# The conditioning products of an eight-head hybrid decoder step, moved from split and plain fp32 on the whole array to plain fp32 on four column strips

## The reference, cut to what matters

```python
def adaln(c, w_ada, b_ada):
    m = jnp.einsum('nd,de->ne', jax.nn.silu(c), w_ada) + b_ada
    return tuple(jnp.split(m[:, None, :], 6, axis=-1))
```

## Time and profile before

| | us |
|---|---|
| median of 3 runs | 1800.78 (1799.39 to 1802.48) |
| the profiled execution, its own time | 1803.02 |
| its span in the trace | 1801.2 |
| PE busy in the span | 1689.8 (94%) |
| DVE, ACT, POOL busy | 1010.5, 739.8, 479.3 |
| stage 1, from the span's start | 0 to 71.8 |
| stage 2 | 71.8 to 294.4 |

### The profile page before, as it was taken

How to read it: one execution, slowest core, us unless ns; L and a number is a source line. 1 busy time by engine, 2 the same in 40 slices (tenths; PEclk the granted TensorE clock), 3 DMA queues, 4 the chain that set the end, 5 groups by cost and what they waited for, 6 DMA issues and landing times. The chain is left out here.

```text
span 1801.2 us, 27774 instructions
## 1 busy us (share of the span) xinstructions
PE 1689.8 (94%) x11308; PEld 1565.1 (87%) x11308; DVE 1010.5 (56%) x1730; ACT 739.8 (41%) x1365; POOL 479.3 (27%) x304
## 2 busy tenths in 40 slices
PE   5799997889999999998999998999999999999997
PEld 2699995788877887876998988999999999999896
DVE  2411113735567877774436464222789778888535
ACT  3311222334555655652324354210474456436511
POOL 0454442100000000000125472221333443434621
PEclk9899997789999999999899999999999999999998
DMA  9254433512111001012562032112020202020422
GB/s 303 66 132 110 106 98 108 152 32 58 38 48 40 29 28 39 29 36 90 171 192 71 36 107 71 36 48 94 12 94 25 71 25 71 25 71 15 139 71 60
DMA packets 174668, 137.16 MB, mean 76 GB/s; under 512 B 44245, under 2 KB 160129, under 8 KB 174505
## 3 DMA queue, kind: packets, MB, share of 16 engines
q1 hardware_dynamic: 166827, 125.16, 23.5%
q10 hardware_dynamic: 7718, 10.29, 1.7%
HBM read 115.82 MB, written 21.92 MB: 76 GB/s over the span
## 5 line engine op out<-in xcount | busy, mean ns | idle before, releaser
L2653 PE MATMUL ff_acc<-x_ring,w_ring 128*128 128x258 f32 x3360 | 407.8, 284 | 3.2 <-DVE x_ring L2954 3.2
L2653 PEld LDWEIGHTS ff_acc<-x_ring,w_ring 128*128 128x128 f32 x3360 | 407.4, 191 | 3.7 <-POOL w_ring L2470 3.0
L2470 POOL TENSOR_TENSOR w_ring<-w_quads,w_ring 128x512 fp32r<-128x512 f32 x90 | 162.5, 1807 | 275.7 <-ACT w_ring L2235 275.6
L1257 PE MATMUL gate_ps<-h_hi,gate_w_cut 128*128 128x344 f32 x768 | 228.5, 346 | 7.4 <-ACT gate_sum L1380 5.1
L2235 ACT ACTIVATE w_ring<-w_quads 128x512 fp32r<-128x512 f32 x140 | 88.1, 629 | 177.1 <-PE ff_acc L2653 86.0
L1257 PEld LDWEIGHTS gate_ps<-h_hi,gate_w_cut 128*128 128x128 f32 x768 | 142.5, 194 | 14.5 <-ACT gate_sum L1380 7.7
L1353 ACT ACTIVATE prob<-scores,bias 128x640 f32<-128x640 f32 (+7 forms) x192 | 106.0, 558 | 99.3 <-DVE bias L1421 50.2
L1448 DVE TENSOR_TENSOR p_lo<-pT,p_hi 128x512 fp32r<-128x512 f32 (+1 forms) x148 | 101.4, 686 | 69.6 <-ACT p_hi L1364 69.1
L1364 ACT ACTIVATE p_hi<-pT 128x512 fp32r<-128x512 f32 (+1 forms) x148 | 88.1, 595 | 99.5 <-PE pT L1307 98.6
L1257 PE MATMUL gate_ps<-h_lo,gate_w_cut 128*128 128x344 f32 x384 | 125.0, 325 | 0.0
L1559 POOL MEMSET qz<- 128x576 f32 x1 | 0.6, 582 | 467.3 <-POOLq L130 467.3
(11 more groups left out here) (424 smaller groups left out, 3922.4 us busy)
## 6 DMA issues: line engine op xcount, KB each, us to landing
w_quads<-in_w_ff_dram SPq DMA_DIRECT2D x20, 1024.0 KB, 5.3
wa_rest<-in_w_ada_dram SPq DMA_DIRECT2D x16, 1024.0 KB, 5.3
gate_spill<-gate_sum SPq DMA_DIRECT2D x48, 172.0 KB, 1.9
gates<-gate_spill SPq DMA_DIRECT2D x16, 516.0 KB, 4.9
wa<-in_w_ada_dram SPq DMA_DIRECT2D x8, 1024.0 KB, 9.8
gate_w_raw<-in_w_in_dram SPq DMA_DIRECT2D x16, 512.0 KB, 4.1
ff_raw<-in_w_ff_dram SPq DMA_DIRECT2D x16, 512.0 KB, 4.1
w_raw<-in_w_in_dram SPq DMA_DIRECT2D x30, 256.0 KB, 6.3
```

What stands on the lines that cost most here:

```text
L1257: last = pe.matmul(gps[:, 0:CH], gw_cut[:, 1 - u % 2, a, k], h[:, k, c * CH:(c + 1) * CH], start=(k == 0 and n == 0), stop=(k == KD - 1 an ...
L2470: pool.tensor_tensor(wr[:, n % HK, 1], quad_piece(ph, W_PART[name], p), wr[:, n % HK, 0].bitcast(F32), ALU.subtract).then_inc(wrest_pool, 1)
L2653: last = pe.matmul(banks[:, 2 * p + c, 0:HC], wr[:, n % HK, a, k], xr[:, jj % 2, b, k, c * HC:(c + 1) * HC], start=(fresh and k == 0 and m ...
```

## The change

Both stages multiply `w_ada` in the same way now, in `strip_products`: plain fp32, with the stationary block padded with zeros from 9 to 32 columns (`c_pad`), and the 8 inner blocks spread over four strips of 32 array columns, two blocks to a strip. Strip s holds the sum of blocks 2s and 2s + 1 in PSUM rows 32s to 32s + 31. The order is: the first block of strips 0, 1, 2, 3, then the second block of strips 0, 1, 2, 3. What the rows' turning multiplies with is a new `fold`, 128 x 9, with a one wherever the row's number modulo 32 is the column's, so that the turning product adds the four strips. Stage 1 turns with this product instead of a transpose. In stage 2 the cuts of `w_ada` on ACT and POOL are gone, and the products wait for the chunk's landing itself.

```diff
+        c_pad = buf.at("c_padded", [P, KD, STRIP], F32, buf.tail + 2 * AC * 4)[0]
+        fold = buf.const("fold", [P, 1 + NS])
+        def strip_products(pe, acc, w_chunk):
+            per = KD // NSTRIP
+            for half in range(per):
+                for strip in range(NSTRIP):
+                    k, row = strip * per + half, strip * STRIP
+                    last = pe.matmul(acc[row:row + STRIP], c_pad[:, k], w_chunk[:, k], start=(half == 0), stop=(half == per - 1),
+                                     skip_group_check=True, tile_position=(0, row))
+            return last
...
-                        for k in range(KD):
-                            last = pe.matmul(adaP[c % 2][:], cT[:, k], wa[:, c % NR, k], start=(k == 0), stop=(k == KD - 1))
+                        last = strip_products(pe, adaP[c % 2], wa[:, c % NR])
...
-                        last = pe.transpose(tp[0][:, n * 16:n * 16 + 1 + NS], arow[:, n * P:(n + 1) * P], ident[0:1 + NS, 0:1 + NS])
+                        last = pe.matmul(tp[0][:, n * 16:n * 16 + 1 + NS], arow[:, n * P:(n + 1) * P], fold[:], start=True, stop=True,
+                                         skip_group_check=True)
...
-                    dve.tensor_copy(cT[:], tp[0][:, 0:KD * 16].rearrange("p (k n) -> p k n", k=KD)[:, :, 0:1 + NS]).then_inc(cT_ready, 1)
+                    dve.memset(c_pad[:, :, 1 + NS:STRIP], 0.0)
+                    dve.tensor_copy(c_pad[:, :, 0:1 + NS], tp[0][:, 0:KD * 16].rearrange("p (k n) -> p k n", k=KD)[:, :, 0:1 + NS]).then_inc(cT_ready, 1)
                     dve.wait_ge(consts_ready, 1)
+                    dve.tensor_reduce(fold[:], ident[:].rearrange("p (s c) -> p c s", s=NSTRIP)[:, 0:1 + NS], AX.X, ALU.add)
...
-                pe.wait_ge(walo_ready, c + 1)
+                pe.wait_ge(wa_loaded[c % 2], 16 * (c // 2 + 1))
                 if c:
                     pe.wait_ge(arow_ready, c)
-                else:
-                    pe.wait_ge(cst_ready, 1)
-                for k in range(KD):
-                    pe.matmul(adaP[:], c_st[:, k], wa_hi[:, k], start=(k == 0), stop=False, skip_group_check=True)
-                    last = pe.matmul(adaP[0:1 + NS], c_st[:, k, 0:1 + NS], wa_lo[:, c % 2, k], start=False, stop=(k == KD - 1),
-                                     skip_group_check=True)
+                last = strip_products(pe, adaP, wa[:, c % 2])
...
-            def cut_ada_hi(act, c):
-                act.wait_ge(wa_loaded[c % 2], 16 * (c // 2 + 1))
...
-            def cut_ada_lo(pool, c):
-                pool.wait_ge(wahi_ready, c + 1)
...
-                    dve.wait_ge(chi_ready, 1)
-                    dve.tensor_tensor(c_st[:, :, 1 + NS:NC2], cT[:], c_st[:, :, 0:1 + NS].bitcast(F32), ALU.subtract)
-                    dve.tensor_tensor(fold[:], ident[0:NC2, 0:1 + NS], ident[0:NC2, 1 + NS:NC2], ALU.add).then_inc(cst_ready, 1)
```

More of the change, by code:

```diff
@@ L282, in hybrid_step @@
         AC = 256
-        cT = buf.const("cT", [P, KD, 1 + NS])
+        STRIP = 32
+        NSTRIP = P // STRIP
+        c_pad = buf.at("c_padded", [P, KD, STRIP], F32, buf.tail + 2 * AC * 4)[0]
[8 more added lines that the diff above has]
+            return last
         with ExitStack() as st:
@@ L290, in hybrid_step @@
             htmp = at("htmp", [P, 4, 512])
-            arow = at("arow", [1 + NS, 2 * D])
+            arow = at("arow", [P, 2 * D])
             sq = at("sq", [P, D])
@@ L298, in hybrid_step @@
             tp = [psum(st, f"tp{i}", [P, 512]) for i in range(3)]
-            adaP = [psum(st, f"adaP{i}", [1 + NS, AC]) for i in range(2)]
+            adaP = [psum(st, f"adaP{i}", [P, AC]) for i in range(2)]
             vec_loaded, c_loaded, xs_loaded = sem("vec_loaded"), sem("c_loaded"), sem("xs_loaded")
@@ L525, in hybrid_step @@
             NA = 4 * D // AC
-            wa_at = at.at[0] - buf.CONSTS - 2 * buf.SLAB
             wa = at("wa_rest", [P, 2, KD, AC])
-            NC2 = 2 * (1 + NS)
-            c_st = at("c_st", [P, KD, NC2], F32R)
-            fold = at("fold", [NC2, 1 + NS])
             assert at.at[0] <= buf.CONSTS + 5 * buf.SLAB
-            wa_lo = buf.slabs(2, wa_at)("wa_rest_lo", [P, 2, KD, AC], F32R)
-            wa_hi = buf.slabs(5, 3 * 8192)("wa_rest_hi", [P, KD, AC], F32R)
             behind_arow = buf.tail
-            arow = buf.small("arow_rest", [NC2, 2, AC])
+            arow = buf.small("arow_rest", [P, 2, AC])
             buf.tail = behind_arow
-            adaP = psum(st, "ada_rest", [NC2, AC])
+            adaP = psum(st, "ada_rest", [P, AC])
             adaT = psum(st, "ada_turned", [P, AC // P, 1 + NS])
@@ L540, in hybrid_step @@
             ada_done, arow_ready, adaT_done, ada_taken = (sem(n) for n in ("ada_rest_done", "arow_rest_ready", "ada_rest_turned", "ada_rest_taken"))
-            wahi_ready, walo_ready, chi_ready, cst_ready = (sem(n) for n in ("wa_rest_hi_ready", "wa_rest_lo_ready", "c_hi_ready", "c_st_ready"))
             def condition(pe, c):
-                pe.wait_ge(walo_ready, c + 1)
+                pe.wait_ge(wa_loaded[c % 2], 16 * (c // 2 + 1))
                 if c:
                     pe.wait_ge(arow_ready, c)
-                else:
-                    pe.wait_ge(cst_ready, 1)
-                for k in range(KD):
-                    pe.matmul(adaP[:], c_st[:, k], wa_hi[:, k], start=(k == 0), stop=False, skip_group_check=True)
-                    last = pe.matmul(adaP[0:1 + NS], c_st[:, k, 0:1 + NS], wa_lo[:, c % 2, k], start=False, stop=(k == KD - 1),
-                                     skip_group_check=True)
+                last = strip_products(pe, adaP, wa[:, c % 2])
                 last.then_inc(ada_done, 1)
@@ L563, in turn_ada @@
                 last.then_inc(adaT_done, 1)
-            def cut_ada_hi(act, c):
-                act.wait_ge(wa_loaded[c % 2], 16 * (c // 2 + 1))
-                if c:
-                    act.wait_ge(ada_done, c)
-                act.activation(wa_hi[:], wa[:, c % 2], ACT.Copy).then_inc(wahi_ready, 1)
-            def cut_ada_lo(pool, c):
-                pool.wait_ge(wahi_ready, c + 1)
-                pool.tensor_tensor(wa_lo[:, c % 2], wa[:, c % 2], wa_hi[:].bitcast(F32), ALU.subtract).then_inc(walo_ready, 1)
             with nc.Block() as block:
@@ L605, in _ @@
                 def _(act):
-                    act.activation(c_st[:, :, 0:1 + NS], cT[:], ACT.Copy).then_inc(chi_ready, 1)
-                    cut_ada_hi(act, 0)
                     for u in range(NU):
@@ L610, in _ @@
                             g.cut_hi(act, u // 2 + 1, u % 2)
-                        cut_ada_hi(act, u + 1)
                 @block.gpsimd
                 def _(pool):
-                    cut_ada_lo(pool, 0)
                     for u in range(NU):
@@ L618, in _ @@
                             g.cut_lo(pool, u // 2 + 1, u % 2)
-                        cut_ada_lo(pool, u + 1)
                 @block.tensor
```

## The result

The changed kernel takes **1778.52 us** (median, 1776.71 to 1780.35) against 1800.88 beside it (1799.39 to 1802.48): ratio 0.9876, 95% interval 0.9861 to 0.989, so 22.4 us less. The profiled execution's span went from 1801.2 to 1778.5.

A forecast was written before the change was run, and what follows sets the result against it. PE was taken to bound stage 2 and the stretch of stage 1 from 29.03 to 49.91 us. Stage 1 -3.2, loop +6.9 and tail -6.7 gave -3.0 us: 1797.8 against the median 1800.78, range 1780 to 1815.

The forecast's parts named there:

- u: Stages 1 and 2: cost of one chunk's products in strips including switching, put at 2.32 us, ends 1.94 and 2.51.
- the loop, 15 units, strips: Stage 2, chunks 0 to 14: products rise from 1.86 to 2.32 us each, 15 x 0.46 = +6.9 us on PE's path.
- the loop, turning over 128 rows: Stage 2: row-turning product keeps its instructions, two products, four passes, 0.52 us, only with 128 rows instead of 18.
- stage 1: Before stage 2: last chunk ends 6.3 us earlier, turning takes 3.1 longer, sum -3.2 us; -5.3 if the clock stays up.
- tail: End of stage 2: PE no longer waits for POOL, but SP is late next; 12.08 - 5.36 = -6.7 us.
- What strips make of it: Strip products: matmuls start in program order, so a chunk takes nine steps of 0.216, 1.94 us, before switching.
- the two bounds, 1.18 and 3.45: A chunk's 16 passes in strips: 1.18 us if all four strips run at once, 3.45 if nothing runs side by side.
- The switch: Stage 2, between whole array and strips: drains and a short exposed load, 0.38 us a chunk, from nothing to 0.57.
- all at once: Rival, chance 0.27: each strip queues its own passes, a chunk costs 1.46 us; -19.0 us, 1781.8.
- loads exposed: Rival, chance 0.13: a strip's second load waits for its first pass, a chunk costs 3.18 us; +13.7 us, 1814.5.
- nothing side by side: Rival, chance 0.15: fp32 passes hold the whole array, a chunk costs 3.83 us; +27.3 us, 1828.1.
- The forecast's own case: Stage 1 with chunk 2 at the lower clock: eighth load released at 35.0, last chunk ends at 43.6; case chance 0.45.

## Why the prediction was wrong

The forecast was -3.0 us; measured -22.4. By its own steps:

| step | forecast | measured | from |
|---|---|---|---|
| u, a chunk's products | 1.86 to 2.32 | 1.86 to 1.00, and 0.10 behind it | timeline after |
| the loop, 15 units, strips | +6.9 | -10.2 | 15 x (13.59 - 12.91) |
| the loop, turning over 128 rows | 0 | -3.9 | 14 x (13.87 - 13.59) |
| stage 1 | -3.2 | -0.1 (to -2.6 in other profiles) | start of stage 2: 71.87, 71.79, 69.29 |
| tail | -6.7 | -6.73 | copy 14 to next stage: 12.33, 5.60 |

In the two profiles: the next stage starts 21.35 us earlier (294.41 to 273.06), of which 14.62 stood by the copy of chunk 14 and 6.73 came behind it; the rest of the span, 1506.8 and 1505.4, is 1.4 shorter. That makes the 22.7 between the spans. The table's rows make 20.9 of the 21.35; the other 0.4 lies in the first unit, which has no turning behind it and leaves the lower level a little sooner after than before.

**The step that failed** is "What strips make of it": PE's matmuls were taken to start in program order across strips, because every row before shows it, and every row before used the array as one. From the two bounds, 1.18 and 3.45, the step went to 1.94 by that order. The runs show that the strips keep only their own order: four rounds of 0.216, 0.86 us without the ends. The lower bound itself was 0.32 too high, since it took the spacing of issue, 0.064 a pair, from the transposes; four passes start within 0.04 us here.

**The switch** was set at 0.38 a chunk. It is 0.14, with 0.10 in the unit behind it, and nearly the same stands where nine columns take the place of strips. Had u been right but for this term, the time would have been 15 x 0.14 = 2.1 us off. (By the forecast's own terms u = 1.94 gives a sum of -8.7, not one below it.)

**The rival "all at once"** had the mechanism, strips that queue their own passes, and 1781.8: 3.3 us above the result. That it came so near in time is luck: its loop, -6.0 against some -14.5, lacked the turning's 3.9 and the smaller u, and its stage 1, -6.3, was too good by 6.2. The rivals "loads exposed" and "nothing side by side" fall with u: the loads lie under the passes though all strips use all rows. Two rules of the Trainium skill (TensorE: Matmul & The Clock Gate, "Part 3: Packing small matmuls — row/col tiling"), strict order of start and overlapping loads only where row groups differ, don't hold here: passes of later strips start ahead of earlier strips' second ones, and 16 loads of 0.11 cost nothing within 1.00.

**The turning** was costed at nothing ("keeps its instructions"). The row for the other price stood among those read, the 0.21 of "issue" before the 18-row load; it was not asked why it was there, nor whether 128 rows would keep it.

**Stage 1.** The eighth load went out at 32.6, as the prediction had it for a clock that stays up, but its chunk began 9.0 us later instead of 6.7 (7.4 to 8.1 in six other profiles with four strips in stage 1 and its turning at the end). The forecast's own case had the load out at 35.0 and landed at 41.7; that the chunk began at 41.62 is luck, two errors that cancel. The forecast saw that PE would wait for it and not what the wait does: the clock at 0.50 through the turning, 6.99 us instead of 4.2. It took 3.1 of added turning where 5.8 came. The start of stage 2 varies by 2.5 us between profiles with this stage 1, with the landing of the last chunk and with the level at which its products run.

**The tail** came out as said: POOL's wait gone, SP last, -6.7. So did three smaller points: the padding and `fold` on DVE, 0.21 and 0.20 us, end by 11.0 us, while the first chunk's products start at 18.02; the mean granted clock in stage 2 is 0.99 from 71.78 to 267.50, as before; and POOL's work in the stage fell from 100.12 to 31.10 us there with no effect but the tail's.

The range, 1780 to 1815, missed by 1.5 us. It ended at the fastest rival, and that rival left out the turning's gain: the working held nothing at which the turning could become cheaper.

## What to carry to other kernels

A product that needs few of the array's columns can go out in strips, also in plain fp32 and in either of the two orders of issue tried here: its cost here is the number of passes in one strip by the spacing of one pass, plus some 0.1 to 0.15 us at the ends. Look for products that use few rows between products that use all; zero rows that fill them up cost nothing here, and gave some 4 us without any other change. Where products become faster than their loads, ask what the array does while it waits: what is issued behind the wait may run at half the clock, and is better placed between the loads (here the next stage started earlier by it, and the whole time didn't show it).

## What the runs showed of the hardware that was not expected

- Four column strips run their fp32 passes side by side, each strip in its own order; rounds are 0.216 us apart, as single passes on the whole array are.
- An 18-row product between 128-row products costs 0.28 us a unit more than the same product filled up to 128 rows. Plain fp32 products of 9, 32 or 64 columns pay 0.10 to 0.15 us at their ends, fp32r products of 9 and 18 columns nothing that shows.
- Within stretches whose granted clock reads 1.00, the same 16 passes took 1.07 us (at 36.12 in the kernel after) and 1.94 us (at 41.08 in the one that turns between chunks). The granted clock alone doesn't tell the pace at the start of a kernel; the spacing does.
- The last of eight equal loads took from 7.4 to 9.0 us from its issue to its chunk's first product in seven profiles with four strips in stage 1 and its turning at the end, one of them (8.1) with no load queued behind it.
